# A two-layer block whose norms' roots move from the products' input to the leaving of PSUM

## The reference, cut to what matters

```python
def rmsnorm_2(x, g):                       # g: one gain per feature
    var = jnp.mean(x * x, axis=-1, keepdims=True)
    return x * lax.rsqrt(var + EPS) * g

def swiglu_ffn(h, w_up, w_down):
    a, b = jnp.split(h @ w_up, 2, axis=-1)
    return (jax.nn.silu(a) * b) @ w_down   # 1024 -> 2 x 2816 -> 1024

for l in range(2):
    x = x + 0.5 * swiglu_ffn(rmsnorm_2(x, norm_ffn1[l]), ...)
    x = x + hybrid_mixer(rmsnorm_2(x, norm_mix[l]), ...)
    x = x + 0.5 * swiglu_ffn(rmsnorm_2(x, norm_ffn2[l]), ...)
return rmsnorm_2(x, final_norm)
```

## Time and profile before

| what | value |
|---|---|
| runs (3) | 2389.42, 2391.83, 2397.37 us; median 2391.83 |
| profiled execution | span 2394.3 us from its first to its last instruction; its time with what lies around it isn't given, and the span is within the range of the runs |
| busy, share of the span | TensorE 87%, its weight loads 69%, VectorE 34%, ScalarE 31%, GpSimd 1% |
| mean granted clock of TensorE | 0.904 of full speed |
| experts (until some 1168 us) | weights stream at 428 to 430 GB/s, TensorE's share is seven or eight tenths |
| layers (from some 1196 us) | 150 to 215 GB/s, TensorE nine tenths or more |

### The profile page before, as it was taken

How to read it: one execution, slowest core, us unless ns; L and a number is a source line. 1 busy time by engine, 2 the same in 40 slices (tenths; PEclk the granted TensorE clock), 3 DMA queues, 4 the chain that set the end, 5 groups by cost and what they waited for, 6 DMA issues and landing times.

```text
span 2394.3 us, 35421 instructions
## 1 busy us (share of the span) xinstructions
PE 2083.8 (87%) x15013; PEld 1643.3 (69%) x15014; DVE 825.7 (34%) x917; ACT 738.0 (31%) x804; POOL 35.5 (1%) x27
## 2 busy tenths in 40 slices
PE   7988877777777776777699999999999999999999
PEld 5858423333333322333499999999999999999998
DVE  4552100000000000000255466764454546676444
ACT  3452100000000000000244347444334334844433
POOL 0000000000000000000000002000000000200000
PEclk7997777888888888878799999999999999999999
DMA  8765699999999999999845654445564565444554
GB/s 302 269 223 228 252 429 429 429 429 428 427 429 429 429 429 428 428 428 429 320 149 165 191 175 176 160 175 184 149 215 152 164 193 170 176 164 171 180 153 126
DMA packets 235215, 657.38 MB, mean 275 GB/s; under 512 B 6933, under 2 KB 121941, under 8 KB 210517
## 3 DMA queue, kind: packets, MB, share of 16 engines
q1 hardware_dynamic: 235092, 655.62, 71.4%
HBM read 654.54 MB, written 1.05 MB: 274 GB/s over the span
## 4 chain that ended last, share of the span: by engine, by line
issue 85%; PE 14%; POOL 1%; DVE 0%; ACT 0%; POOLq 0%; DVEq 0%; ACTq 0%
PE psum L1106 4%; PE psum L1107 4%; PE psum L1108 4%; POOL work L699 0%; PE psum L1050 0%; POOL work L700 0%; POOL work L698 0%; PE psum L1130 0%; PE psum L1129 0%; PE psum L1128 0%; DVE h L2088 0%; PE psum L1061 0%; PE psum L1173 0%; ACT ring_r L1403 0%; POOL work L701 0%
## 5 line engine op out<-in xcount | busy, mean ns | idle before, releaser
L1106 PE MATMUL psum<-work_r,ring_r 128*128 128x256 f32 x2912 | 824.5, 283 | 0.1
L1108 PE MATMUL psum<-work_r,ring_r 128*128 128x256 f32 x2912 | 823.4, 283 | 0.0
L1868 DVE TENSOR_TENSOR ring_r<-ring,ring_r 128x2048 fp32r<-128x2048 f32 (+2 forms) x182 | 450.0, 2505 | 334.8 <-ACT ring_r L1403 334.8
L1106 PEld LDWEIGHTS psum<-work_r,ring_r 128*128 128x128 f32 x2912 | 558.2, 192 | 0.6 <-DVE work_r L2053 0.5
L1108 PEld LDWEIGHTS psum<-work_r,ring_r 128*128 128x128 f32 x2912 | 558.1, 192 | 0.0
L1107 PE MATMUL psum<-h_lo,ring_r 128*128 128x256 f32 x1856 | 525.2, 283 | 0.0
L1403 ACT CAST ring_r<-ring 128x2048 fp32r<-128x2048 f32 (+2 forms) x182 | 363.7, 2040 | 325.6 <-PE psum L1108 324.8
L1107 PEld LDWEIGHTS psum<-h_lo,ring_r 128*128 128x128 f32 x1856 | 356.3, 192 | 0.1
L1107 PE MATMUL psum<-work_r,ring_r 128*128 128x256 f32 x1056 | 298.6, 283 | 0.0
L1002 PE MATMUL psum<-ring,work 128*32 128x512 f32 x1536 | 216.0, 718 | 42.9 <-DMA ring<-in_w_up_e_dram 41.0
L1024 PE MATMUL psum<-ring,work 128*32 128x512 f32 x768 | 125.9, 790 | 88.6 <-DMA ring<-in_w_down_e_dram 88.5
(11 more groups left out here) (272 smaller groups left out, 1955.6 us busy)
## 6 DMA issues: line engine op xcount, KB each, us to landing
ring<-in_w_gate_e_dram SPq DMA_DIRECT2D x64, 2048.0 KB, 12.4
ring<-in_w_down_e_dram SPq DMA_DIRECT2D x48, 2048.0 KB, 31.7
ring<-in_ffn_w_up_dram SPq DMA_DIRECT2D x41, 2048.0 KB, 7.8
ring<-in_w_up_e_dram SPq DMA_DIRECT2D x32, 2048.0 KB, 21.4
work<-in_w_up_e_dram SPq DMA_DIRECT2D x32, 2048.0 KB, 30.2
ring<-in_w_in_dram SPq DMA_DIRECT2D x26, 2048.0 KB, 7.9
ring<-in_ffn_w_down_dram SPq DMA_DIRECT2D x32, 1408.0 KB, 7.1
work<-in_w_down_e_dram SPq DMA_DIRECT2D x16, 2048.0 KB, 37.5
```

The lines of the kernel that those rows point to most:

```text
L1106: pe.matmul(out_b, w_hi[:, k, cols], hi[:, tokens], start=(k == 0), stop=False)
L1108: mm = pe.matmul(out_b, w_lo[:, k, cols], hi[:, tokens], start=False, stop=(k == n_k - 1))
L1868: dve.tensor_tensor(lo_unit(name, unit), raw_unit(name, unit), hi_unit(name, unit).bitcast(F32), ALU.subtract).then_inc(lo_ready, 1)
```

## The change

Products take x times the norm's gain, split into high and low part, without the root; the group that leaves PSUM is multiplied by the root on VectorE.

- ScalarE's `next_input` rounds x * gain to the high part and squares x, and VectorE's `low` takes the low part, chunk by chunk, while x is being finished. VectorE sums all eight squares (`add_square`).
- `mean_square`, one f32 product of 256 columns with 1/1024 in all 128x128 places, stands between the two blocks of `first_projections`; its result is the mean square on every partition. ScalarE's `layer_root` (256 columns) and VectorE's `norm` (reciprocal of 256 columns into rstd_row) follow. Column sums, spreading products and both sets of warm-up products of a norm go. Before the first layer 3 x 14 warm-up products stay.
- The groups a, lru, gelu, pool and g are emptied by VectorE (`scaled`: times rstd_row, to SBUF), and ScalarE applies silu, gelu, sigmoid or the convolution's first tap in place from SBUF. Down products are scaled by 0.5 and the root into `scaled_out`, and a second VectorE instruction adds them to x.
- The order of both engines in the mixer changes, as the diff shows.
- The entry: VectorE rounds tile upa 0 0. ScalarE waits at the head of the loop body for the layer's columns. VectorE marks the banks as free after its low parts and sums.
- The end: high and low part of x * gain are transposed by products with a rounded identity while the last chunks finish, and the root of each token (now on partitions) is applied in the last evictions.

```diff
@@ TensorE
-            def norm(n, alone, dst, w, b=6):
...
-                mm.then_inc(l_ms, 1)
-                keep_warm(dst, w, WARM)
-                spread_columns(l_rstd, n + 1, bank[7], TT, l_spread)
-                keep_warm(dst, w, WARM)
+            def mean_square(n, buffer):
+
+                pe.wait_ge(l_sum, n)
+                pe.matmul(bank[6][:, 0:S], mean_d[:].broadcast_to([P, P]), squares[buffer][:, 0, :],
+                          start=True, stop=True).then_inc(l_ms, 1)
 
             pe.wait_ge(lo_ready, splits.ready(("upa", 0, 0), 0, 0))
-            norm(0, 1, bank[2], hi_unit(("upa", 0, 0), 0), 0)
+            keep_warm(bank[2], hi_unit(("upa", 0, 0), 0), 3 * WARM)
...
                     for b in range(2):
+                        if b:
+                            mean_square(3 * l + (i + 1), i == 2)
...
-                    if f == 0:
-                        next_norm(3 * l + 1, 7, ("lru", 0), ("proj", 1), l)
-                    else:
-                        next_norm(3 * l + 3, 7, ("a", 0, 0), ("upa", 0, 0), l + 1)
...
-                next_norm(3 * l + 2, 6, ("a", 1, 0), ("upa", 1, 0), l)
...
+            pe.wait_ge(ident_r_ready, 1)
+            for c in range(KD):
+                pe.wait_ge(h_lo_ready, 8 * 3 * LAYERS + c + 1)
+                for t in range(TT):
+                    out_t = bank[2 * t + c // 4][:, P * (c % 4):P * (c % 4 + 1)]
+                    pe.matmul(out_t, h_hi[:, c, P * t:P * (t + 1)], ident_r[:], start=True, stop=False)
+                    mm = pe.matmul(out_t, h_lo[:, c, P * t:P * (t + 1)], ident_r[:], start=False, stop=True)
@@ ScalarE
-            split(("upa", 0, 0), 0)
-
             act.activation(table[:], mean_d[:], ACT.Sqrt)
...
+            def next_input(k, gain, buffer):
+
+                act.activation(h_hi[:, k, :], x[:, k, :], ACT.Identity, scale=gain).then_inc(h_hi_ready, 1)
+                act.activation(squares[buffer][:, k, :], x[:, k, :], ACT.Square).then_inc(l_sq, 1)
+
+            def layer_root(n, buffer):
+                act.wait_ge(l_ms, n)
+                act.activation(squares[buffer][:, 1, :], bank[6][:, 0:S], ACT.Sqrt, bias=EPS).then_inc(l_std, 1)
...
+                act.wait_ge(cols_layer, l + 1)
+                ffn(0, 0, ("proj", 1), gain_of("norm_mix"))
...
-                h_high(1)
                 split(("proj", 2), l)
+                layer_root(3 * l + 2, 0)
+                split(("proj", 3), l)
                 lru_input(0)
                 lru_input(1)
-                split(("proj", 3), l)
+                split(("proj", 0), l)
                 lru_input(2)
                 lru_input(3)
-                split(("proj", 0), l)
+                split(("proj", 4), l)
                 lru_input(4)
                 gelu(0)
-                for g in range(2):
-                    src = done(("pool", g))
-                    act.copy(pool_u[:, 2 * g:2 * g + 2, 16:], src.rearrange("p (c t) -> p c t", c=2)).then_inc(emptied["act"], 1)
-                split(("proj", 4), l)
@@ VectorE
+                def scaled(dst, group):
+
+                    src = done(group).rearrange("p (c t) -> p c t", c=2)
+                    dve.tensor_tensor(dst, src, rstd_row[:].unsqueeze(1).broadcast_to([P, 2, S]),
+                                      ALU.mult).then_inc(emptied["dve"], 1)
...
                     for j in range(5):
                         split(("upb", f, j), l)
+                        if j == 0:
+                            norm(3 * l + (i + 1), i == 2)
+                        scaled_flat(silu_a[:, (2 * j) % 4, :], ("a", f, 2 * j))
+                        scaled_flat(silu_a[:, (2 * j + 1) % 4, :], ("a", f, 2 * j + 1))
...
-                        dve.scalar_tensor_tensor(out=x[:, c, :], in0=src[:, 0:S], scalar=0.5, in1=x[:, c, :], op0=ALU.mult,
-                                                 op1=ALU.add).then_inc(emptied["dve"], 1)
-                    wait_emptied(("dn", f, KD - 1))
+                        dve.scalar_tensor_tensor(out=scaled_out[:, c % 2, :], in0=src[:, 0:S], scalar=0.5, in1=rstd_row[:],
+                                                 op0=ALU.mult, op1=ALU.mult).then_inc(emptied["dve"], 1)
+                        wait_emptied(("dn", f, c))
+                        dve.tensor_tensor(x[:, c, :], x[:, c, :], scaled_out[:, c % 2, :], ALU.add).then_inc(l_x, 1)
+                    dve.wait_ge(l_x, l * 16 + (8 * f + KD))
+                    low(n, KD - 1, gain(KD - 1))
+                    add_square(n, KD - 1, 0)
...
                 split(("proj", 2), l)
+                norm(3 * l + 2, 0)
+                lru_scaled(0)
+                lru_scaled(1)
+                split(("proj", 3), l)
                 conv(0)
-                split(("proj", 3), l)
                 conv(1)
+                lru_scaled(2)
+                lru_scaled(3)
+                split(("proj", 0), l)
                 conv(2)
-                split(("proj", 0), l)
                 conv(3)
+                lru_scaled(4)
+                gelu_scaled(0)
+                split(("proj", 4), l)
                 conv(4)
-                split(("proj", 4), l)
+                for g in range(2):
+                    scaled(pool_u[:, 2 * g:2 * g + 2, 16:], ("pool", g))
...
                 split(("pup", 0), l)
+                gate_scaled(6)
+                gate_scaled(7)
                 dve.wait_ge(pool_mix_hi_ready, l + 1)
                 dve.tensor_tensor(pool_mix_lo, pool_mix.rearrange("p c t -> p (c t)"), pool_mix_hi.bitcast(F32),
                                   ALU.subtract).then_inc(pool_mix_lo_ready, 1)
```

More of the change, by code:

```diff
@@ L1084, in wait_emptied @@
                     pe.wait_ge(emptied[e], n)
-                def next_norm(n, alone, group, tile_name, layer):
-                    e, value = groups.bank_free(group, layer)
-                    pe.wait_ge(emptied[e], value)
-                    pe.wait_ge(lo_ready, splits.ready(tile_name, 0, layer))
-                    norm(n, alone, bank[groups.bank(group)], hi_unit(tile_name, 0))
                 def three_passes(group, tile_name, unit, hi, lo, blocks, before_k=None, first=0):
@@ L2020, in _ @@
                 split(("proj", 8), l)
+                gate_scaled(2)
+                gate_scaled(3)
                 dve.wait_ge(mult_ready, l + 1)
@@ L2069, in _ @@
                     for q in (2 * i, 2 * i + 1):
-                        for k in range(max(1, 2 * q - 4), 2 * q - 2):
-                            add_square(3 * l + 2, k, 5)
+                        for k in range(2 * q - 2, 2 * q):
+                            if k >= 0:
+                                low(3 * l + 2, k, gain_of("norm_ffn2")(k))
+                            if k >= 1:
+                                add_square(3 * l + 2, k, 1)
                         src = done(("out", q))
```

228 lines of the change are left out of this document (122 added, 106 removed).

## The result

The changed kernel takes **2374.32 us** (median of four runs, 2370.62 to 2380.17) against 2393.57 for the kernel before (four runs on the same chip, 2389.42 to 2397.37). The ratio is 0.992, with a 95% interval from 0.990 to 0.994: faster by 0.6 to 1.0%. The change is clear of the noise, but small. The profiled execution took 2372.06 us with a span of 2370.3, so 1.8 us lie around the span.

A forecast was written before the change was run, and what follows sets the result against it. TensorE, busy 87% of the span, was taken as the bound, with only gaps between full stretches to win. Gains of 42.4 us less losses of 25.0 gave 17.4 net: 2374.4 us, range 2357 to 2387.

The forecast's parts named there:

- The norms' gaps: TensorE's idle gaps at the norms, 5.5 to 11.0 us each, go whole: 38.3 us gained.
- The f32 product's price: One f32 product of 256 columns in each first projection, 0.44 us each, six of them: 2.7 us lost.
- The mixer's queues: Tile 4's split stands ahead of other mixer work; TensorE stops before ra 4: 6.15 us lost a layer, 16.3 with clock.
- The clock term of the mixer: Products after the mixer's stop run at the low clock: 2.0 us lost a layer, bounds 0 and 5.
- The loop's end: TensorE's 3.46 us branch at the end of the layer loop is no longer hidden: 1.8 us lost, once.
- pup: TensorE waits before pup because gate_scaled(7) precedes the pooled mix's low part on VectorE: 2.1 us a layer, 4.2 lost.
- The entry: Before the first layer, TensorE starts at 1193.5 instead of 1196.2 but loses 1.9 at low clock: net 0.8 us gained.
- The end: From last product to last eviction, 9.2 us shrinks to between 5.2 and 6.4: 3.3 us gained.
- (a): Rival: the mixer's new waits are hidden, so the 16.3 us are not lost: 2358 us, chance 0.12.
- (b): Rival: VectorE and GpSimd are later than reckoned, 13.4 us less gain: 2387.8 us, no change to tell, chance 0.14.
- (c): Rival: each new stop leaves TensorE at its low clock, 48 us instead of 5.9: 2416 us, chance 0.05.
- (d): Rival: the norms' gaps do not close, chunks 6 and 7 come 2 us late at five norms: 2384 us, chance 0.04.

The follow-up runs named there:

- order_act: Changed kernel with only ScalarE's split of projection tile 4 put back behind lru_input(4) and gelu(0): 2370.05 us, layers' time 1204.6.
- order_both: Changed kernel with the split of projection tile 4 put back on ScalarE and, behind the pool evictions, on VectorE: 2362.10 us, layers' time 1194.7.
- order_late: Changed kernel with ScalarE's split of projection tile 4 put back and VectorE's moved behind the pooled values: 2354.90 us, layers' time 1188.5.
- order_dve: Changed kernel with only VectorE's split of projection tile 4 put back behind conv(4) and the pool evictions: 2390.69 us, layers' time 1223.5.
- warm_stops: Changed kernel with more warm-up products: 50 at the entry, 48 before ra 4, 16 before the pup wait: 2389.12 us, layers' time 1214.2.
- warm_wait: warm_stops with GpSimd's long multiplication in the mixer made to wait for the pooled values: 2366.64 us, layers' time 1200.5.
- pe_unrolled: Changed kernel with TensorE's loop over the two layers written out: 2371.86 us, layers' time 1198.8.
- pup_first: Changed kernel with the low part of the pooled mix ahead of gate_scaled(7) on VectorE: 2366.45 us, layers' time 1199.2.
- all_five: order_late plus TensorE's loop written out, the entry's bank mark before the sums, and pup's low part before both gates: 2339.07 us, 0.978 of the kernel before.

## Why the prediction was right, point by point

The median came out at 2374.32 where 2374.4 was written, and that is closer than the terms deserve. Against the kernel before, whose median is 2393.57 with its fourth run, the gain is 19.3 us; by the layers' time it is 16.8 us (18.2 by order_act's) against 17.4. And the sum holds because errors cancel: the mixer lost 4.8 us less than written, the loop's end 2.3 and slow products elsewhere 2.7 more. That part is luck. Term by term:

**The norms' gaps.** Right, all 38.3 us. The third norm's rows above show 0.12 us where 7.1 stood. The f32 product's price is right too: the segment from P 6 to the last product grew by 0.42, with 0.45 expected, and it has nothing else in it.

**The mixer's queues.** Right in mechanism and place: VectorE's split ahead of conv(4) and the evictions; a stop of 6.4 where 6.5 was worked out, GpSimd's additions 5.6 us undisturbed (5.7), the segment 6.2 longer (6.6). order_act, order_both and order_late show it. Two things in this part failed. The pooled values let TensorE wait 0.5 us in one layer and 1.0 in the other, not 2 to 3. (The profile puts the 1.0 down to ScalarE's last sigmoid, which ended within 0.03 us of them; pmix's bank had long been free.) And the prediction had no idea how near GpSimd's multiplication stood to VectorE's pooling; 0.4 us earlier in the second layer or 0.9 in the first, and by the rows of order_dve it would have held up the last of that pooling for over 5 us, as it did the second operation in order_dve and warm_stops.

**The clock term of the mixer, 2.0 a layer.** Wrong in place. ra 4 to ix 4 did run slowly (0.81 mean over the 18 us), 7.96 instead of 5.45 us, but they end at 1443.07, before the pooled values at 1443.42, so the 2.5 us cost nothing: the slower engine was not the one waited for. (In the five traces with this stop they took 7.2 to 8.0 us and the segment was 66.5 or 66.6 each time; warm_wait ran them at the full clock, and its second layer's segment is 66.5, too.) The clock's price came elsewhere: 14 slow products at the loop's end (1.3 us) and 15 behind the second layer's pup stop (1.4), 2.7 us in all, which the prediction had not counted; in the mixer it had 4.0 where nothing came.

**The loop's end.** Mechanism right, size wrong: 4.1 us stood where 1.8 was written, because the branch took 5.69 us and not the 3.46 of the row. The difference, 2.23, is the miss. pe_unrolled shows that the branch is the cause. The Trainium skill, page Advanced Engine Details and Errata (Control Flow Timing), with its 108 ns, fits only the branch that falls through (83 ns).

**pup.** 2.25 a layer, 2.1 expected. The words "which no order of arrival can hide" and "3 us of slack" were wrong: half of it is VectorE's own lateness (pup_first), and with the low part ahead of both gates 0.2 of the stop remain (all_five).

**The entry.** P 1 came 3.2 us earlier (2.7) and its first products cost 2.2 at the low clock (1.9): net 1.0, 0.8 expected. But the same entry takes 2 us less in five other traces, whose column sums ran at the full clock, so this agreement is partly luck.

**The end.** 9.3 to 6.0, as written. The root is a column now and takes VectorE 0.17 us, and the evictions that apply it follow at once, two on VectorE and two on ScalarE:

```profile
2364.89 0.17 DVE L2126 RECIPROCAL rstd_col<-std 128x2 f32<-128x2 f32 x1 [1.83 <-ACT std L1562]
2365.09 1.41 DVE L2130 TENSOR_SCALAR work<-psum,rstd_col 128x512 f32<-128x512 f32 x2
```

**The rivals.** (a), waits hidden, needs a split that doesn't wait for pool 1: the 12.09 us of [ACT ring_r L1382] exclude it. (b), VectorE and GpSimd late, was near without happening: its GpSimd half is order_dve. (c) had the clock cost 48 us; the slow products cost 2.2 + 1.3 + 1.4 = 4.9, and warm_stops, which kept the clock up at the entry, gained 2.3 there at most. The page TensorE: Matmul & The Clock Gate of the Trainium skill (HAM oscillation) has stops bring the clock down; by the slow products they did after the entry's and the loop's stops of 3.8 us and more in every trace, and after 9 of the 14 stops of 2.1 to 2.25 us before pup in the seven traces that have them. (d) is excluded by the windows in which TensorE is busy without a pause.

## What to carry to other kernels

When work moves from one engine to another, read the order of the receiving queue before anything else: of some 25 us that this change lost (2.7 for f32 products, 11.5 in the mixer, 4.5 before pup, 4.1 at the loop, 2.7 of slow products), 16 were places in a hand-written queue, and five small edits gave back 33 us of the layers' time, some 3 of them the entry's scatter. A wait in front of an instruction delays all that stands behind it, so place a late-released operation behind what others wait for. And before speeding an engine up, look what its end releases: an operation of GpSimd with two inputs in SBUF may come to stand beside such a one of VectorE's, and one of them then waits until the other ends.

## What the runs showed of the hardware

- A 16-column operation of VectorE took 5.56 us beside a 2560-column one of GpSimd, 0.17 alone. GpSimd's additions took 3.96 instead of 1.99, 3.46 instead of 1.53 and, in order_both, 3.00 instead of 1.07: 1.9 to 2.0 more each, where half a split is 2.25. VectorE's evictions out of PSUM weren't lengthened beside the multiplication (0.53 and 0.54 us).
- TensorE's jump back over a long loop took 3.46 and 3.59 us in the kernel before, 5.59 to 5.87 in seven traces with the changed kernel's loop and 4.12 and 4.52 with more products on the loop; it repeats within 0.3 us for one loop and isn't explained.
- The experts' part, alike in all kernels, ended at 1163.6 to 1165.7 us in eight of the fourteen traces and at 1171.2 to 1173.2 in the other six, never between. What chooses isn't known. A difference of single runs under 10 us says nothing here, while the layers' time repeated within 0.1 us for the kernel before. In changed kernels the clock moves it by up to 3 us at the entry and by some 1.5 behind each pup stop.
- After stops of 2.1 to 2.25 us (pup) 15 to 17 products ran 0.21 us apart in nine cases of fourteen, from up to 1.4 us after the stop's end on; in the other five all ran at 0.12. After 3.0 us at warm_wait's loop end none was slow, after 2.6 us at warm_stops' 16 were. The low level of the two clocks is not a function of the stop's length alone.
